# Attention's take-outs first in two queues, and the convolution's output projection in two halves of the contraction

## Chip, cores and metric

The kernel runs on one core of one Trainium2 chip. The metric is the device time of one execution in microseconds; the time of a kernel is the median of several runs. One further execution is taken with the hardware profiler, and all rows of the trace come from it.

## What is computed

Two decoder layers on 512 tokens of width 1024, in float32. Cut to what matters here:

```python
h = h + attention(rms_norm(h))     # layer 0: 16 query heads, 2 key/value heads, window 128,
                                   # softmax with a learned sink per head, then @ w_o
h = h + moe(rms_norm(h))           # 32 experts, top group of 4, then 2 of its 8 experts
h = h + gated_short_conv(rms_norm(h))                 # layer 1
h = h + moe(rms_norm(h))
out = rms_norm(h)

def gated_short_conv(h, w_in, conv_w, w_out):
    b_gate, c_gate, u = split(h @ w_in, 3)            # w_in: 1024 x 3072
    z = c_gate * u
    conv = sum(shift(z, 2 - j) * conv_w[j] for j in range(3))
    return (b_gate * conv) @ w_out                    # w_out: 1024 x 1024, contraction over 1024
```

## The kernel before, in words

Five engines run in-order programs of their own and hand over by semaphores: PE (matmuls), DVE and ACT (elementwise work, both read PSUM), POOL and SP (SP issues nearly all DMAs, in order). A product of two float32 matrices that must be exact is made of three matmuls on rounded parts (split_product, L833): each operand is split into a high part, written by ACT (L634), and a low part, written by DVE (L1247).

**Attention** goes by 8 units u, a block of 128 queries and one key/value head (8 query heads) each. Per unit PE makes scores (att_scores, L881), transposes the probabilities in four steps (att_turn, L901), multiplies by the values (att_out, L914) into bank 6, and, one unit behind, projects the heads of unit u - 1 in two halves of the columns (project_heads, L833) into bank 7. PE's order in unit u: scores(u+2), turn(u) steps 0 and 1, project_heads(u-1) half 0, turn(u) steps 2 and 3, project_heads(u-1) half 1, att_out(u). att_out's result is taken out of bank 6 in two steps, ACT's high part (att_take_out, L678) and then DVE's low part (L1309), and project_heads waits for the second. The queues around it: DVE does att_bias(u+2) (scores plus bias and their maximum, L1281 and three small steps, L1285 to L1287), att_take_out(u-1), add_heads (h += bank 7, L1317), att_scale(u+1) (L1297 to L1302), add_heads; ACT does att_exp(u+1) (L650, L653), att_scale(u) (L664), att_take_out(u-1), att_turn(u) (copies of the transposes, L670). The last units also hold the first steps of the next norm: root (ACT, L591, L596) and norm_tile (DVE, L1201), turned by PE (turn_tile, L819).

**The expert stages** stream the weights of 32 experts through a ring of 8 slots of 2 MB, laid over the buffers big, small, arena and xt. SP fills a slot when the product that used it is done (load_experts, L411); the first 8 fills of a layer wait for what held the buffer before, by the list early_free. The products are L1063 (gate and up) and L1081 (down).

**The convolution** makes h @ w_in in 8 gate blocks j of 128 columns of each of the three gates: 72 matmuls into banks 3(j%2) to 3(j%2)+2. w_in comes in four quarters of 256 columns through big[0] and big[1], w_out behind them (L459). For each block ACT copies the c gate out (L793) and splits the weights of block j + 2; DVE makes z, the three-tap convolution and the product with the b gate (L1541 to L1546), writes its high and low parts into gated and gated_low (L1547, L1548, conv_ready) and splits block j + 2. w_out's eight row blocks are split behind gates 6 and 7. When the last gate's DVE steps are done, project multiplies: for each of 4 token tiles t and 2 halves of the columns, f = 2t + half, 24 matmuls over the whole contraction into bank 6 + f%2. DVE adds the bank to h (L1360, mix_used), ACT and DVE norm the tile, PE turns it (turn_tile) and makes the router's logits (L974), woven between the products.

## Time and profile before

| | |
|---|---|
| median of 3 runs | 1422.33 us (1418.08 to 1423.3) |
| the profiled execution | 1416.9 us, span 1415.0 us |
| PE busy | 1259.5 us, 89% of the span |
| DVE, ACT, POOL busy | 410.2, 325.6, 153.7 us |
| DMA | 456.17 MB, mean 322 GB/s |
| chain that ended last | PE 63%, DMA 26%, DVE 7%, ACT 2% |

The span in 40 equal slices of 35.4 us; a digit is a busy share in tenths, PEclk the granted clock of TensorE:

```profile
PE   5978798999999999988389998999999999998891
DVE  6454453112111111111445454321112111111114
ACT  3235542211211112111331121112122111211112
POOL 5650030000000000000000000201000000000000
PEclk8989999999999999999679999999999999999996
DMA  9200635999999999999922232399999999999995
```

Slices 1 to 7 are attention, 7 to 19 the first expert stage, 21 to 26 the convolution, 27 to 39 the second expert stage. In the timelines a row has start, length, engine, line, operation and operands, and in brackets the idle time of the engine before it and what ended it. A matmul's end is modelled, so its length overlaps the next one's; a short one of 128x512 is listed with 0.39 us and followed after 0.23.

### The profile page before, as it was taken

The numbers are of one execution on the slowest core, as the hardware profiler recorded it, in microseconds if no ns is written. First come the engines' busy times: TensorE is split into PE (matmuls) and PEld (weight loads), VectorE is DVE, ScalarE is ACT, GpSimd is POOL, SyncE is SP. The second block draws the span as 40 slices with busy tenths as digits, with TensorE's granted clock in tenths as the row PEclk, the third lists the DMA queues.
The fourth block names the chain that finished last, engine by engine and source line by source line (L and its number), as shares of the span: only waits on it lengthen the run. The fifth ranks groups of instructions, "written<-read, shape, count | busy, mean of one in ns | idle before, by whom it ended". The sixth has DMA issues, their size and how long they took to land.

```text
span 1415.0 us, 15354 instructions
## 1 busy us (share of the span) xinstructions
PE 1259.5 (89%) x6042; PEld 672.2 (48%) x6042; DVE 410.2 (29%) x871; ACT 325.6 (23%) x620; POOL 153.7 (11%) x125
## 2 busy tenths in 40 slices
PE   5978798999999999988389998999999999998891
PEld 4756564444443433333168886744444434333330
DVE  6454453112111111111445454321112111111114
ACT  3235542211211112111331121112122111211112
POOL 5650030000000000000000000201000000000000
PEclk8989999999999999999679999999999999999996
DMA  9200635999999999999922232399999999999995
GB/s 351 86 0 1 244 150 240 427 428 426 429 428 428 429 426 429 428 427 427 340 44 89 89 119 119 125 427 426 428 426 428 429 428 427 429 427 427 428 422 212
DMA packets 63859, 456.17 MB, mean 322 GB/s; under 512 B 14852, under 2 KB 30238, under 8 KB 39236
## 3 DMA queue, kind: packets, MB, share of 16 engines
q1 hardware_dynamic: 52436, 444.29, 75.4%
q0 software_dynamic: 5120, 8.41, 1.6%
q10 hardware_dynamic: 6256, 2.80, 0.8%
q8 instruction: 34, 0.56, 0.2%
q14 instruction: 13, 0.11, 0.0%
HBM read 444.96 MB, written 18.90 MB: 328 GB/s over the span
## 4 chain that ended last, share of the span: by engine, by line
PE 63%; DMA 26%; DVE 7%; ACT 2%; issue 1%; POOLq 0%; DVEq 0%; ACTq 0%
PE ps L833 20%; PE ps L1063 20%; PE ps L1081 11%; DMA xt<-in_moe_w_gate_up_dram 10%; DMA big<-in_moe_w_gate_up_dram 10%; PE ps L1040 6%; DMA xt<-in_moe_w_down_dram 5%; PE ps L1053 1%; DVE xr L1201 1%; PE ps L1072 1%; PE ps L974 1%; PE ps L1048 1%; PE ps L914 1%; PE ps L819 1%; PE ps L881 1%
## 5 line engine op out<-in xcount | busy, mean ns | idle before, releaser
L1063 PE MATMUL ps<-big,arena 128*64 128x512 f32 x1024 | 228.1, 594 | 21.4 <-DMA big<-in_moe_w_gate_up_dram 20.7
L1452 DVE TENSOR_TENSOR gain<-arena,ps 64x512 f32<-64x512 f32 x64 | 68.7, 1073 | 432.9 <-ACT arena L721 432.9
L528 POOL DMA_INDIRECT rows<-arena x64 | 62.5, 977 | 880.6 <-DVE arena L1478 880.6
L721 ACT ACTIVATE arena<-ps 64x512 f32<-64x512 f32 x64 | 37.7, 590 | 518.7 <-PE ps L1063 518.7
L1063 PEld LDWEIGHTS ps<-big,arena 128*64 128x64 f32 x1024 | 72.3, 137 | 171.5 <-issue 136.2
L1063 PE MATMUL ps<-small,arena 128*64 128x512 f32 x512 | 114.9, 594 | 10.6 <-DMA small<-in_moe_w_gate_up_dram 10.6
L833 PE MATMUL ps<-xt_parts,small_parts 128*128 128x512 f32 x288 | 113.9, 405 | 6.9 <-DVE big L1260 5.4
L1081 PE MATMUL ps<-big,arena 128*64 128x512 f32 x512 | 116.9, 598 | 0.0
L833 PE MATMUL ps<-xr_parts,small_parts 128*128 128x512 f32 x272 | 108.5, 399 | 0.0
L833 PE MATMUL ps<-xt_parts,big_parts 128*128 128x512 f32 x256 | 101.6, 397 | 0.0
L1040 PE MATMUL ps<-arena_parts 128*128 128x512 f32 x256 | 83.6, 408 | 3.1 <-DVE arena_parts L1448 3.1
L1040 PE MATMUL ps<-xr_parts,arena_parts 128*128 128x512 f32 x256 | 80.0, 394 | 0.0
L1063 PEld LDWEIGHTS ps<-small,arena 128*64 128x64 f32 x512 | 36.1, 137 | 86.4 <-issue 67.5
L1478 DVE COPY arena<-ps 128x512 f32<-128x512 f32 x64 | 44.3, 692 | 96.4 <-PE ps L1081 96.0
L833 PEld LDWEIGHTS ps<-xt_parts,small_parts 128*128 128x128 f32 x288 | 56.5, 196 | 20.5 <-issue 6.8
L1081 PEld LDWEIGHTS ps<-big,arena 128*64 128x64 f32 x512 | 33.9, 136 | 63.1 <-issue 63.1
L1063 PE MATMUL ps<-arena 128*64 128x512 f32 x256 | 57.8, 594 | 5.3 <-DMA arena<-in_moe_w_gate_up_dram 5.3
L1477 DVE CAST arena<-arena 128x2 int32<-128x2 f32 x32 | 5.4, 169 | 196.9 <-PE ps L1081 196.9
L1063 PE MATMUL ps<-xt,arena 128*64 128x512 f32 x256 | 57.9, 594 | 5.1 <-DMA xt<-in_moe_w_gate_up_dram 5.1
L707 ACT ACTIVATE arena<-ps 128x512 f32<-128x512 f32 x64 | 34.7, 594 | 113.9 <-PE ps L1040 113.9
L819 PE MATMUL ps<-ident,xr 128*128 128x128 f32 x128 | 23.1, 342 | 40.9 <-DVE xr L1201 40.9
L1081 PE MATMUL ps<-small,arena 128*64 128x512 f32 x256 | 58.5, 598 | 0.8 <-DMA small<-in_moe_w_down_dram 0.8
(169 smaller groups left out, 1518.5 us busy)
## 6 DMA issues: line engine op xcount, KB each, us to landing
big<-in_moe_w_gate_up_dram SPq DMA_DIRECT2D x64, 2048.0 KB, 29.0
small<-in_moe_w_gate_up_dram SPq DMA_DIRECT2D x32, 2048.0 KB, 29.6
big<-in_moe_w_down_dram SPq DMA_DIRECT2D x32, 2048.0 KB, 32.8
xt<-in_moe_w_gate_up_dram SPq DMA_DIRECT2D x16, 2048.0 KB, 29.8
arena<-in_moe_w_gate_up_dram SPq DMA_DIRECT2D x16, 2048.0 KB, 30.1
small<-in_moe_w_down_dram SPq DMA_DIRECT2D x16, 2048.0 KB, 32.8
arena<-in_moe_w_down_dram SPq DMA_DIRECT2D x8, 2048.0 KB, 32.7
xt<-in_moe_w_down_dram SPq DMA_DIRECT2D x8, 2048.0 KB, 34.7
```

The source lines that it names most:

```text
L528: nc.gpsimd.indirect_dma_start(out=rows_dram[l], out_offset=bass.IndirectOffsetOnAxis(ap=where[:, j:j + 1], axis=0), in_=y_rows[:, j, :], ...
L707: nc.scalar.activation(picked[:, half * HALF:(half + 1) * HALF], ps[half][:], ACT.Copy)\
L721: nc.scalar.activation(silu[BLOCK:P, j, :], ps[2 + j][0:BLOCK, :], ACT.Silu).then_inc(S.silu_ready, 1)
L819: mm = nc.tensor.transpose(ps[f % 4][:, a * P:(a + 1) * P], xr[:, t, d * P:(d + 1) * P], ident[:])
L833: mm = nc.tensor.matmul(bank, parts(a), parts(b), start=start and a is left and b is right, stop=stop and a is left_low)
L881: mm = nc.tensor.matmul(ps[bank][:, col:col + hi * P], queries(n)[r0:r0 + HD, j, :], keys[r0:r0 + HD, g, (TT - 1 - n) * P:(TT - 1 - n + hi ...
L914: mm = nc.tensor.matmul(ps[6][half * HD:(half + 1) * HD, :], values[:, TT - 1 - n + c, g * HD:(g + 1) * HD], probsT[:, half * 4:half * 4 + ...
L1040: mm = nc.tensor.matmul(ps[half][:], parts(sel[:, t].rearrange("p j s -> p (j s)")), parts(x[:, t, half * HALF:(half + 1) * HALF]), start= ...
L1063: mm = nc.tensor.matmul(ps[2 + j][half * BLOCK:(half + 1) * BLOCK, :], xg[:, k, j * BLOCK:(j + 1) * BLOCK], w[:, a, half * FF:(half + 1) * ...
L1081: mm = nc.tensor.matmul(ps[6 + j][half * BLOCK:(half + 1) * BLOCK, :], hidT[:, j, k, :], w[:, k, half * HALF:(half + 1) * HALF], start=(k ...
L1452: V.tensor_tensor(hid[BLOCK:P, j, :].rearrange("q (k p) -> q p k", p=P), silu[BLOCK:P, j, :].rearrange("q (p k) -> q p k", p=P), ps[2 + j] ...
L1478: V.tensor_copy(y_rows[:, j, :], ps[6 + j][:]).then_inc(S.row_ready[j], 1)
```

## The change

1. Attention. On DVE att_take_out(u-1) stands ahead of att_bias(u+2). On ACT it stands first in the unit; att_exp(u+1) is cut in two halves of four heads, each ahead of two of the four copies of att_turn(u), and att_scale(u+1) comes last. Before the first unit, ACT scales unit 0 ahead of exp(1). At the end norm_tile(1,1) and root(1,1) stand ahead of the last take-out.
2. Convolution. The contraction of the output projection is cut in two. The first half (gate blocks 0 to 3) is multiplied behind gate block 5 (tile 0), 6 (tile 1) and 7 (tiles 2 and 3), and DVE adds it to h (add_first_half); project then multiplies the second half and adds again. w_out comes in two parts, its first half into rows of big that quarters 0 and 1 of w_in leave free, ahead of quarter 2 in SP's queue. Its splits stand behind gates 3, 6 and 7.
3. Expert ring of layer 1: the slots are in another order, with other early releases.
4. ACT's Square writes its unused output to another place (squares_at), since the arena is laid out anew.

```diff
-gated = cut(DT, T)
-gated_low = cut(DT, T)
+gated_parts = cut(2, 2, FT, T)
...
+out_high = cut(2, D)
...
 ring = [[halves[1][0], small[:, 0], halves[0][1], halves[0][0], late_slot, halves[1][1], small[:, 1], xt_slot],
-        [*halves[1], *halves[0], small[:, 0], small[:, 1], late_slot, xt_slot]]
+        [*halves[1], halves[0][1], small[:, 1], late_slot, halves[0][0], small[:, 0], xt_slot]]
...
+def first_half_bank(f):
+    return ps[half_banks[f]][:]
+half_banks = [6, 7, 6, 7, 6, 7, 0, 1]
...
 def out_weights(k):
-    at = 2 * CONV_W + k * D if k < 2 else (k - 2) * D
-    return big[:, QUARTERS % BIG_SLOTS, k, :], spare[:, at:at + D]
...
+    if k < 2:
+        return big[:, 0, 6 + k, :], spare[:, 2 * CONV_W + k * D:2 * CONV_W + (k + 1) * D]
+    if k < FT:
+        return big[:, 1, 4 + k, :], out_high[:, k - 2, :]
+    return big[:, 0, k - FT, :], spare[:, (k - FT) * D:(k - FT + 1) * D]
...
+SPLIT_ORDER = [("in", 0), ("in", 1), ("in", 2), ("in", 3), ("in", 4), ("in", 5),
+               ("out", 0), ("out", 1), ("out", 2), ("out", 3), ("in", 6), ("in", 7),
+               ("out", 4), ("out", 5), ("out", 6), ("out", 7)]
+def out_splits(j):
+    return {3: range(FT), DT - 2: range(FT, DT - 1), DT - 1: range(DT - 1, DT)}.get(j, [])
+def conv_split_at(what, n):
+    return CONV_SPLIT + SPLIT_ORDER.index((what, n))
...
             [(mix_ps, 4 * TT)] * 2 + [(logits_ps, TT)] if l == 0 else \
-            [(gates_ps, DT)] * 2 + [(mix_ps, 6 * TT)] * 5 + [(logits_ps, 2 * TT)]
+            [(gates_ps, DT)] + [(mix_ps, 6 * TT)] * 4 + [(mix_ps, 8 * TT)] * 2 + [(logits_ps, 2 * TT)]
...
+        if q == BIG_SLOTS:
+            for s in range(2):
+                sp.dma_start(big[:, s, 6:8], w_out[0, 2 * s * P:2 * (s + 1) * P, :].rearrange("(k p) n -> p k n", p=P))\
+                    .then_inc(w_out_in, 16)
...
     sp.wait_ge(gates_ps, (QUARTERS - BIG_SLOTS + 1) * QC // P)
-    sp.dma_start(big[:, QUARTERS % BIG_SLOTS], w_out[0].rearrange("(k p) n -> p k n", p=P)).then_inc(w_out_in, 16)
+    sp.dma_start(big[:, 0, 0:FT], w_out[0, FT * P:D, :].rearrange("(k p) n -> p k n", p=P)).then_inc(w_out_in, 16)
...
-            act.wait_ge(mix_used, TT * (i + 1) + 2 * t + 2)
+            act.wait_ge(mix_used, 4 * TT * (i // 2) + 2 * TT + 2 * t + 2)
...
-        nc.scalar.activation(x_high[:, t] if i % 2 else squares_at, h[:, t, :], ACT.Square,
+        nc.scalar.activation(squares_at, h[:, t, :], ACT.Square,
...
-    def att_exp(u):
+    def att_exp(u, half):
         b = u % 3
-        act.wait_ge(peak_ready, u + 1)
         hi = P if unit(u)[0] == 0 else 2 * P
-        nc.scalar.activation(sink_e[:, b, :], sink_e[:, b, :], ACT.Exp).then_inc(sink_ready, 1)
-        for k in range(HG):
+        if half == 0:
+            act.wait_ge(peak_ready, u + 1)
+            nc.scalar.activation(sink_e[:, b, :], sink_e[:, b, :], ACT.Exp).then_inc(sink_ready, 1)
+        for k in range(half * HG // 2, (half + 1) * HG // 2):
...
-    att_exp(0)
+    att_exp(0, 0)
+    att_exp(0, 1)
+    att_scale(0)
     for u in range(U):
-        if u + 1 < U:
-            att_exp(u + 1)
-        att_scale(u)
         if u >= 1:
             att_take_out(u - 1)
-        if u == U - 1:
+        if u + 1 < U:
+            att_exp(u + 1, 0)
+        att_turn(u, (0, 1))
+        if u + 1 < U:
+            att_exp(u + 1, 1)
+        else:
             root(1, 0)
-        att_turn(u)
+        att_turn(u, (2, 3))
+        if u + 1 < U:
+            att_scale(u + 1)
+    root(1, 1)
     att_take_out(U - 1)
-    for t in range(1, TT):
+    take_turned(1, 0)
+    for t in range(2, TT):
         root(1, t)
         take_turned(1, t - 1)
     take_turned(1, TT - 1)
...
+    def split_out(j):
+        for k in out_splits(j):
+            act.wait_ge(w_out_in, 16 * 2 if k < FT else 16 * 3)
+            if k >= FT:
+                act.wait_ge(gates_ps, DT - 1 if k < DT - 1 else DT)
             split_high(*out_weights(k))
...
-        if j == DT - 2:
-            act.wait_ge(w_out_in, 16)
-            split_out(range(5))
-        if j == DT - 1:
-            split_out(range(5, DT))
+        split_out(j)
...
-            for ks in ([range(5), range(5, DT)] if t == 0 else [range(DT)]):
+            for ks in ([range(FT, DT - 1), range(DT - 1, DT)] if t == 0 else [range(FT, DT)]):
                 for half in range(2):
                     f = 2 * t + half
-                    if f >= 2:
-                        pe.wait_ge(mix_used, first + f - 1)
+                    pe.wait_ge(mix_used, first + f - (1 if f >= 2 else 3))
                     for k in ks:
                         mm = product(ps[6 + f % 2][:], t, half, k)
                     if k == DT - 1:
...
+    def conv_product(bank, t, half, k):
+        if t == 0 and half == 0:
+            pe.wait_ge(w_split, conv_split_at("out", k) + 1)
+        w, high = out_weights(k)
...
-        pe.wait_ge(w_split, CONV_SPLIT + j + 1)
+        pe.wait_ge(w_split, conv_split_at("in", j) + 1)
...
+        if j == 5:
+            pe.wait_ge(conv_ready, FT)
+        for t in {5: [0], 6: [1], 7: [2, 3]}.get(j, []):
+            for half in range(2):
+                f = 2 * t + half
+                if t == TT - 1:
+                    pe.wait_ge(conv_ready, DT - 1)
+                elif t >= 1:
+                    pe.wait_ge(mix_used, 4 * TT + f - 1)
+                for k in range(FT):
+                    mm = conv_product(first_half_bank(f), t, half, k)
+                mm.then_inc(mix_ps, 1)
     pe.wait_ge(conv_ready, DT)
-    project(4 * TT, 3, conv_product)
+    project(6 * TT, 3, conv_product)
...
     take_queries(4, ps[7])
-    att_scale(0)
+    att_scale(0, (0, 1))
     att_bias(2)
     take_queries(5, ps[7])
+    att_scale(1, (0,))
     take_queries(6, ps[7])
-    att_scale(1)
+    att_scale(1, (1,))
     take_queries(7, ps[7])
     dve.wait_ge(h_biased, TT)
     for u in range(1, U):
         g, t = divmod(u - 1, TT)
+        att_take_out(u - 1)
         if u + 2 < U:
             att_bias(u + 2)
-        att_take_out(u - 1)
         add_heads(g, t, 0)
         if u + 1 < U:
-            att_scale(u + 1)
+            att_scale(u + 1, (0, 1))
         else:
             norm_tile(1, 0)
         add_heads(g, t, 1)
+    norm_tile(1, 1)
     att_take_out(U - 1)
-    norm_tile(1, 1)
     take_turned(1, 0)
...
-                dve.wait_ge(mix_ps, 2 * TT * (l + 1) + f + 1)
+                dve.wait_ge(mix_ps, 4 * TT * l + 2 * TT + f + 1)
...
+    def add_first_half(t):
+        for half in range(2):
+            f = 2 * t + half
+            dve.wait_ge(mix_ps, 4 * TT + f + 1)
+            hs = h[:, t, half * HALF:(half + 1) * HALF]
+            V.tensor_tensor(hs, first_half_bank(f), hs, ALU.add).then_inc(mix_used, 1)
...
     for j in range(DT):
         b = j % 2
+        if j == DT - 1:
+            add_first_half(1)
...
-            split_low(CONV_SPLIT + j + 2, *conv_weights(j + 2))
-        for k in (range(5) if j == DT - 2 else range(5, DT) if j == DT - 1 else []):
-            split_low(CONV_SPLIT + DT + k, *out_weights(k))
+            split_low(conv_split_at("in", j + 2), *conv_weights(j + 2))
+        for k in out_splits(j):
+            split_low(conv_split_at("out", k), *out_weights(k))
+        for t in {6: [0], 7: [2, 3]}.get(j, []):
+            add_first_half(t)
```

mix_ps and mix_used count 16 in attention, 8 in the first half and 8 in the second, where they counted 8 for the whole projection; root, add_mix and early_free are adapted to that.

## Rows read from the trace of the kernel before

**Rows 1.** Chain that ended last, in order of time: start, length, what.

```profile
229.49 13.95 PE ps L1063 x64
...
679.02 3.68 PE ps L1081 x16
...
856.53 18.04 PE ps L833 x72
...
932.35 13.95 PE ps L1063 x64
...
1382.91 3.68 PE ps L1081 x16
```

**Rows 2.** Waits of PE, 98 to 200 us: total, times, longest.

```profile
PE ps L833 <- DVE xr_parts L1309: 14.1, 7, 4.1
PE ps L833 <- issue: 2.4, 1, 2.4
PE ps L819 <- DVE xr L1201: 1.0, 1, 1.0
```

**Rows 3.** Timeline of PE, first projection matmul of attention units 4 and 7.

```profile
147.86 0.47 PE L833 MATMUL ps<-small_parts,xt_parts 128*128 128x512 f32 x1 [2.91 <-DVE xr_parts L1309]
...
184.37 0.47 PE L833 MATMUL ps<-small_parts,xt_parts 128*128 128x512 f32 x1 [0.49 <-DVE xr_parts L1309]
```

**Rows 4.** Timeline of DVE in unit 4.

```profile
143.66 0.42 DVE L1281 CUSTOM_DVE_ANT_0 arena<-ps,arena 128x256 f32<-128x256 f32 x1 [2.36 <-PE ps L881]
...
147.03 0.68 DVE L1309 TENSOR_TENSOR xr_parts<-ps,xt_parts 128x512 fp32r<-128x512 f32 x1
```

**Rows 5.** Groups by line, ACT and DVE, 128 to 170 us: busy us, mean ns.

```profile
L653 ACT ACTIVATE big<-big,arena 128x256 f32<-128x256 f32 x8 | 3.9, 502 | 0.0
L670 ACT ACTIVATE arena<-ps 128x512 f32<-128x512 f32 x12 | 6.5, 595 | 17.9 <-PE ps L901 17.9
...
L664 ACT ACTIVATE big<-big,arena 128x256 f32<-128x256 f32 x4 | 1.7, 498 | 0.0
...
L1302 DVE TENSOR_TENSOR big<-big,arena 128x1024 f32<-128x1024 f32 x1 | 1.2, 1226 | 0.0
```

**Rows 6.** Stretches: length, engines' busy us, then PEclk, DMA share, GB/s.

```profile
105.60:109.00 3.40, 3.33 (x9) 2.67 (x10) 0.02 (x1) 0.00 (x0) 0.00 (x0) 0.56 0.00 0
173.00:177.00 4.00, 4.00 (x13) 3.02 (x12) 0.00 (x0) 0.00 (x0) 0.00 (x0) 0.57 0.99 422
856.50:860.50 4.00, 3.97 (x11) 3.21 (x12) 3.50 (x3) 0.00 (x0) 0.00 (x0) 0.62 1.00 426
```

**Rows 7.** Timelines of ACT, DVE and PE at gates 6 and 7.

```profile
835.26 4.84 ACT L634 ACTIVATE small_parts<-big 128x1024 fp32r<-128x1024 f32 x5
...
835.47 0.69 DVE L1541 TENSOR_TENSOR arena<-arena,ps 128x512 f32<-128x512 f32 x1 [8.23 <-ACT arena L793]
...
840.20 5.77 DVE L1247 TENSOR_TENSOR big_parts<-big,small_parts 128x1024 fp32r<-128x1024 f32 x5
851.79 0.69 DVE L1541 TENSOR_TENSOR arena<-arena,ps 128x512 f32<-128x512 f32 x1 [5.83 <-ACT arena L793]
...
856.53 0.80 PE L833 MATMUL ps<-small_parts,arena_parts 128*128 128x512 f32 x1 [5.48 <-DVE arena_parts L1548]
```

**Rows 8.** Timeline of DVE behind the projection of tile 0.

```profile
869.16 0.69 DVE L1360 TENSOR_TENSOR h<-ps,h 128x512 f32<-128x512 f32 x1 [1.35 <-PE ps L833]
871.47 0.16 DVE L1194 RECIPROCAL rstd<-rstd 128x1 f32<-128x1 f32 x1 [1.61 <-ACT rstd L596]
871.67 2.07 DVE L1201 SCALAR_TENSOR_TENSOR xr<-h,rstd,gain 128x1024 f32<-128x1024 f32 x1
```

**Rows 9.** Timelines of DVE and POOL at the end of attention.

```profile
195.25 3.16 DVE L1201 SCALAR_TENSOR_TENSOR xr<-h,rstd,gain 128x1024 f32<-128x1024 f32 x1
...
194.21 2.40 POOL L542 TENSOR_TENSOR xr_parts<-xr,arena_parts 128x1024 fp32r<-128x1024 f32 x1
```

**Rows 10.** Timeline of SP's issues at the end of the convolution.

```profile
851.08 57.84 SPq L411 DMA_DIRECT2D big<-in_moe_w_gate_up_dram  x4
```

More of the change, by code:

```diff
@@ L665, in att_scale, with att_turn @@
                                          scale=rden[:, b, k:k + 1]).then_inc(scaled_act, 1)
-            def att_turn(u):
-                for f in range(4):
+            def att_turn(u, fs):
+                for f in fs:
                     act.wait_ge(pT_ps, 4 * u + f + 1)
@@ L775, in split_conv @@
                 split_high(*conv_weights(j))
-            def split_out(ks):
-                for k in ks:
-                    out_weights_wait(act, k)
+            def split_out(j):
[3 more added lines that the diff above has]
+                        act.wait_ge(gates_ps, DT - 1 if k < DT - 1 else DT)
                     split_high(*out_weights(k))
@@ L1154, in _ @@
             turn(2)
+            def conv_product(bank, t, half, k):
+                if t == 0 and half == 0:
+                    pe.wait_ge(w_split, conv_split_at("out", k) + 1)
+                w, high = out_weights(k)
+                cols = slice(half * HALF, (half + 1) * HALF)
+                rows = slice(t * P, (t + 1) * P)
+                return split_product(bank, gated(k)[:, rows], gated_low(k)[:, rows], high[:, cols], w[:, cols],
+                                     k % FT == 0, k % FT == FT - 1)
             for j in range(DT):
                 w, high = conv_weights(j)
-                pe.wait_ge(w_split, CONV_SPLIT + j + 1)
+                pe.wait_ge(w_split, conv_split_at("in", j) + 1)
                 if j >= 2:
@@ L1164, in _ @@
                 mm.then_inc(gates_ps, 1)
-            def conv_product(bank, t, half, k):
-                if t == 0 and half == 0:
-                    pe.wait_ge(w_split, CONV_SPLIT + DT + k + 1)
-                w, high = out_weights(k)
-                cols = slice(half * HALF, (half + 1) * HALF)
-                rows = slice(t * P, (t + 1) * P)
-                return split_product(bank, gated[:, k, rows], gated_low[:, k, rows], high[:, cols], w[:, cols],
-                                     k == 0, k == DT - 1)
+                if j == 5:
[10 more added lines that the diff above has]
+                        mm.then_inc(mix_ps, 1)
             pe.wait_ge(conv_ready, DT)
-            project(4 * TT, 3, conv_product)
+            project(6 * TT, 3, conv_product)
             router(1)
@@ L1293, in att_scale @@
                 dve.wait_ge(sink_ready, u + 1)
-                for half in range(2):
+                for half in halves:
                     heads = slice(half * 4, half * 4 + 4)
@@ L1357, in add @@
                             take_turned(2 * l + 1, t - 1)
-                        dve.wait_ge(mix_ps, 2 * TT * (l + 1) + f + 1)
+                        dve.wait_ge(mix_ps, 4 * TT * l + 2 * TT + f + 1)
                         hs = h[:, t, half * HALF:(half + 1) * HALF]
                         V.tensor_tensor(hs, ps[6 + f % 2][:], hs, ALU.add).then_inc(mix_used, 1)
-                    dve.wait_ge(mix_used, 2 * TT * (l + 1) + 2 * t + 2)
+                    dve.wait_ge(mix_used, 4 * TT * l + 2 * TT + 2 * t + 2)
                 return add
@@ L1546, in _ @@
                 step(V.tensor_tensor(conv, conv, ps[3 * b][:], ALU.mult))
[L1547 to L1548 removed]
+                step(V.tensor_copy(parts(gated(j)), conv))
+                V.tensor_tensor(parts(gated_low(j)), conv, parts(gated(j)), ALU.subtract).then_inc(conv_ready, 1)
                 dve.wait_ge(conv_ready, j + 1)
                 if j + 2 < DT:
[L1551 to L1553 removed]
+                    split_low(conv_split_at("in", j + 2), *conv_weights(j + 2))
[3 more added lines that the diff above has]
+                    add_first_half(t)
             norm(3, add_mix(1))
```

11 lines of the change are left out of this document (5 added, 6 removed).

## Prediction

> **What bounds the kernel now.** I read the chain that ended last first, in order of time, because it cuts the run into stages with different limits. From 229.49 to 679.02 (first expert layer) and from 932.35 to 1382.91 (second) it runs through expert products and, from the second half on, waits for expert weights [rows 1]: there the DMA is the limit, and I take such a stage as a block of fixed length behind its first product. The blocks are 679.02 - 229.49 = 449.53 us and 1382.91 - 932.35 = 450.56 us. So the change is worth what it moves the first expert product of each layer, plus what it changes in a block. The two stretches that it edits lie ahead: attention (to 229.49) and the convolution (to 932.35).
>
> In attention the waits of PE come next: 14.1 us in 7 waits for the take-out on DVE (L1309), and 2.4 us in one before a project_heads, with no releaser named, which by the code is the same wait (unit 5) [rows 2]. The timelines say why. In unit 4 PE has scores and transposes done near 145.0 and starts project_heads at 147.86, after 2.91 us [rows 3]. ACT's take-out stands behind exp and scale in its queue. DVE's stood behind att_bias, which began at 143.66 when the scores were there, and ran only at 147.03 [rows 4].
>
> In the convolution the chain is the gate blocks' and the projection's matmuls (8 x 72 and 192 by the code), with one stop of PE, 5.48 us before 856.53, for the last gate's DVE steps [rows 7]. A gate block of 72 matmuls takes 851.79 - 835.47 = 16.32 us, 0.227 us each at full clock [rows 7].
>
> **Attention, step by step.** With the take-outs first on ACT and DVE, the path from att_out's end to project_heads is ACT 0.6, DVE 0.7 and three hand-overs. Together that is 1.5 us. Unit 7, where nothing stands ahead of the take-outs and PE has only 1 us of transposes beside them, shows it: 0.49 us of wait are left [rows 3]. Units 1 to 5 have scores and transposes of over 2 us beside it, so their waits go to zero; unit 6, unit 7 and the last product keep 0.49 each. The waits sum to 14.1 + 2.4 = 16.5, so 16.5 - 1.5 = 15.0 us go.
>
> What is late next, counted from att_out's end in a middle unit: DVE takes out to 1.4, att_bias (2.9 + 0.6) to 4.9, the add of the first half at 5.8, scale (one step of 1.2 and four small ones) to 8.4. ACT takes out to 0.7, exp's first half (one small step, four of 3.9 / 8 = 0.49) to 2.8, two copies (0.54 each) to 4.1, exp's second half to 6.0, the other two copies, released by PE's transposes at about 6.7, to 7.2, scale (1.7) to 10.1 [rows 5]. PE's own work is 11.5 (10 for the shortest). att_out needs the copies at 9.5, the next unit's transposes need scale's first half at 13.4 and its second at 17. So PE stays the limit, with 2 us to spare at the tightest point. The exps are now queued behind a take-out that waits for PE, and PE's transposes wait for them; this slack is their cover, and without it they cost what is missing per unit. In unit 1 the add (behind att_bias and its GpSimd delays) should hold the second half by 0.5 us.
>
> PE's clock: behind the longest of these waits (4.1 us [rows 2], unit 1) the stretch 105.6 to 109.0 had a granted clock of 0.56, and behind unit 6's the stretch 173 to 177 had 0.57 [rows 6]. Losses of 3.4 x 0.44 + 4 x 0.43 = 3.2 us, at the 1.2 GHz level. I take the whole as regained; the bounds are 0 and 3.2.
>
> The end: norm_tile(1,1) moves ahead of DVE's last take-out. It then runs from 192.1, before GpSimd's subtraction (194.21) starts, in the 2.07 us that the same step takes alone, in place of the 3.16 that it took beside it [rows 8, 9]. The take-out comes 0.5 us later, the wait of 1.0 before turn_tile(1,1) goes [rows 2], and the following steps come about 0.7 us earlier in all. The Trainium skill (SBUF — State Buffer, Who interferes with whom) has it that a VectorE instruction with two SBUF inputs and a GpSimd one that reads SBUF block each other by issue order; these rows agree. By it this edit would be worth up to the whole 1.1 us, which moves the sum by 0.4.
>
> Attention: -15.0 + 0.5 - 3.2 - 0.7 = **-18.4 us** (bounds -14 to -20). The first layer's ring is then loaded no later relative to its first product: its seven early slots are released by events that move along, so its block stays at 449.5.
>
> **Convolution.** The product work is the same: 8 x 12 + 8 x 12 matmuls for 192. Loads: 2 MB of w_out go ahead of quarter 2 of w_in in SP's queue, and so delay it by some 5 us (5.2 to 12.8 was the landing time of such issues); DVE's split of block 4 ends near 778 and PE takes it at 786, so nothing is lost. The first four w_out splits, 4 x 0.97 on ACT and 4 x 1.15 on DVE [rows 7], fill the idle 8 us of DVE behind gate 3. add_first_half adds 8 DVE adds of 0.69 [rows 8]; 4 lie behind products, 4 behind the last gate, all while PE multiplies.
>
> The gain: behind block 7 PE has tiles 2 and 3, 48 x 0.227 = 10.9 us, where it stood 5.48. Gone are the stop and the slow matmuls after it: 72 took 18.04 against 16.32 [rows 1], about 1.6 without the pipeline's tail, with the clock at 0.62 [rows 6]. Together -7.0.
>
> The new wait: tile 1's first half, behind block 6, goes into bank 6, which still holds tile 0's. PE waits for mix_used 17, the add of tile 0. That add stands in DVE's queue at the end of gate 6, which can't begin before block 6 ends. Queued ahead of it: the gate's steps (its first begins at 835.47, 0.7 behind the block's end at 834.8, and the splits behind its last at 840.20: 5.4 us), then three splits of 1.15 (5.77 for 5), then the add itself, 0.69, and 0.1 to PE: 5.4 + 3.5 + 0.7 + 0.1 = **9.7 us** [rows 7, 8]. Behind the waiting PE stand tile 1, block 7 and all after it. DVE's splits wait for ACT's, 0.6 + 3 x 0.97 after the block, which is in time. A stop of 9.7 us costs at least the slow start of the 5.5 us one, 1.6 us. Together +11.3.
>
> The second half, 12 matmuls (2.7 us) for a bank instead of 24 (5.4), turns the norm into a wait. From a product's end to xr: the add begins 0.2 later, then 0.7, ACT's root 1.6, DVE 2.3 (0.2 and 2.07) [rows 8], 4.8 us. Before, PE had 5.4 (tile 0) or more beside it. Now turn_tile(0) waits 1.8, the next two 0.3 each. Together +2.4.
>
> Convolution: -7.0 + 11.3 + 2.4 = +6.7; written out from block to block I get tile 3's last product at 914.5 instead of 907.9, so **+6.6 us** (bounds +4, if the adds overlap better, to +10, with a second loss of clock).
>
> **Second expert block.** SP could issue two slots at 851.08 and then stood for 57.84 us [rows 10]. Now it issues one there, four with the first half done and two at the end; all eight are in SBUF before the first expert product. The first block (449.53) is the case in which they were, so **-1.0 us** (0 to -1.5). Three slots more beside the projection are otherwise worth nothing: the ring is full anyway until PE frees a slot.
>
> **Sum.** -18.4 + 6.6 - 1.0 = -12.8. Span 1415.0 to 1402.2. The profiled execution was 1416.9, 1.9 above its span, which gives 1404.1; it lay 5.4 below the median of the three runs, 1422.33. For a median of runs I take 1422.33 - 12.8 = 1409.5.
>
> **Rivals.** (A) The bank is free in time, and PE does not stop behind block 6. For it: two banks in turn. Against: the order of the DVE program, above. Then -18.4 - 7.0 + 2.4 - 1.0 = -24.0, 1398. The Trainium skill (Perfetto Trace Analysis, Matmuls) says that independent groups rotating through banks let the evacuation of one overlap the next group's matmuls; read by it alone this would happen. No row here shows an add of a first half; the trace bears out only that a released bank costs no wait.
> (B) ACT becomes the limit of a unit: exps behind the take-out push its last copies past the second half's end, and att_out waits. The slack is 2 us; were it missed by 1.4 us in each of six units, 8 us of the 18.4 are lost: -4.4, 1418. Against: ACT's busy time is about 8.6 of 11.5 us.
> (C) Slower: PE stays at 1.2 GHz after the 9.7 us stop, held there by the short stops of the second half. 24 + 72 + 48 + 96 = 240 matmuls follow, 0.2 us dearer each: 48 us, so 1422.3 - 12.8 + 48, about 1458. It is slower than before from 64 of these matmuls on. Against: after the 5.48 us stop the full clock was back in about 4 us: 11 matmuls there, where 17 fit at full clock, and only 1.7 us lost in 72 [rows 1, 6].
> (D) The moves don't act in attention, since PE's true limit there is another: 0 + 6.6 - 1.0, 1428.
>
> **Chances.** Forecast 0.69, A 0.09, B 0.14, C 0.03, D 0.05. Under 0.5% (7.1 us) this kernel's runs can't tell a change from none. The forecast's own range is 1402 to 1417, from the bounds above and the spread of the three runs; with A at one end and B at the other, 1398 to 1418. Faster by over 0.5%: most of the forecast and A, 0.77. Within: B and the rest of the forecast, 0.16. Slower: 0.07.
>
> **What would show it.** Waits of PE for L1309's successor of about 0.5 us, three times, in place of 16.5 us; first expert product near 211; behind gate block 6 one stop of 9 to 10 us, ended by a DVE add of h; none behind block 7; waits of 1 to 2 us before the first turned tile of the second half; first to last expert product 449 to 450 us in both layers; SP issuing four ring slots together before the second half. Wrong if PE stops longer than 1 us in units 2 to 6, or not at all behind block 6.

## Result, and the profile after

| kernel | median us | ratio to before, 95% interval | span of the profiled execution |
|---|---|---|---|
| before | 1420.2 (4 runs, 1417.94 to 1423.3) | | 1415.0 |
| after | 1404.05 (4 runs, 1401.89 to 1406.87) | 0.9886 [0.9856, 0.9916] | 1400.2 |

The change makes the kernel 16.2 us faster by the medians; the two profiled executions differ by 14.8 us.

The page of after, its parts 2 (granted clock in 40 slices) and 4 (chain by engine):

```profile
PEclk9999999999999999999599989999999999999996
...
PE 63%; DMA 27%; DVE 8%; ACT 1%; issue 1%; POOLq 0%; DVEq 0%; ACTq 0%
```

The shares hardly move; in the clock the 5 is the norm ahead of the convolution, and the 8 behind it the stop told of below. The chain in order of time (start, length, what) has the same stages as [rows 1]:

```profile
209.96 13.95 PE ps L1094 x64
...
659.45 3.68 PE ps L1112 x16
...
698.12 121.63 PE ps L865 x528
825.21 3.50 DVE big_parts L1291 x3
829.36 40.30 PE ps L865 x165
...
918.46 13.95 PE ps L1094 x64
...
1367.83 3.68 PE ps L1112 x16
```

Cut at the first and last expert product of each layer, for these two and for the kernels of the experiments that need it:

| us | before | after | att_only | conv_only | add_first | ring_late |
|---|---|---|---|---|---|---|
| to the first expert product | 229.49 | 209.96 | 208.40 | 234.08 | 208.23 | 213.06 |
| first block | 449.53 | 449.49 | 449.46 | 449.48 | 449.55 | 449.53 |
| norm, convolution, router | 253.33 | 259.01 | 253.15 | 260.61 | 248.96 | 261.02 |
| second block | 450.56 | 449.37 | 450.77 | 449.37 | 449.38 | 455.68 |

After against before: -19.5 in attention, +5.7 in the convolution, -1.2 in the second block and 0.3 more behind the last product make -14.8. The first block did not move.

Two of these stages hold a difference that is no work of the change. The 16 products of the pick, the last PE work of a router, take about 3.9 us at a granted clock of 1.00 and 5.5 us at a mean of 0.70. In attention they were slow in after and fast in before (3.91 us) and att_only (3.89); behind the convolution they were fast in after (3.87 us) and slow in before (5.49). The row of after in attention:

```profile
201.95 5.49 PE ps L1071 x16
```

With equal picks the change gives -21.1 in attention and +7.3 in the convolution, which are the values of att_only and conv_only; the 1.6 us cancel in the sum.

**Attention.** PE's waits from 80 to 200 us (total, times, longest), of the kernel after:

```profile
PE ps L865 <- DVE xr_parts L1353: 1.6, 3, 0.6
PE ps L865 <- DVE h L1361: 0.9, 2, 0.5
```

L1353 is the take-out, L1309 of before: 1.6 us in three waits where there were 16.5 in eight [rows 2]. DVE's timeline shows the take-out standing ahead of att_bias, and the product that waited 2.91 us [rows 3] starting without a pause, in PE's timeline:

```profile
131.86 0.69 DVE L1353 TENSOR_TENSOR xr_parts<-ps,xt_parts 128x512 fp32r<-128x512 f32 x1 [1.81 <-ACT xt_parts L704]
132.46 0.41 DVE L1325 CUSTOM_DVE_ANT_0 arena<-ps,arena 128x256 f32<-128x256 f32 x1
```
```profile
133.45 0.47 PE L865 MATMUL ps<-small_parts,xt_parts 128*128 128x512 f32 x1
```

**Convolution.** PE's waits from 820 to 920 us, then DVE at gate 6 and PE's first matmul after the stop, then a stretch behind it (the last three columns are PEclk, DMA share and GB/s):

```profile
PE ps L865 <- DVE h L1588: 9.6, 1, 9.6
PE ps L851 <- DVE xr L1245: 1.7, 2, 1.4
```
```profile
825.21 3.50 DVE L1291 TENSOR_TENSOR big_parts<-big,small_parts 128x1024 fp32r<-128x1024 f32 x3
828.62 1.28 DVE L1588 TENSOR_TENSOR h<-ps,h 128x512 f32<-128x512 f32 x2
...
829.36 0.80 PE L865 MATMUL ps<-small_parts,arena_parts 128*128 128x512 f32 x1 [9.61 <-DVE h L1588]
```
```profile
829.30:833.50 4.20, 4.14 (x10) 3.28 (x11) 0.60 (x2) 0.00 (x0) 0.00 (x0) 0.50 0.00 0
```

This is the predicted stop: the bank of tile 0's first half comes free only when the add has had its turn behind the gate's six steps and three splits. No stop is left behind gate block 7. The price can be read from ACT's c gates, which follow a block's end at once: 853.93 - 819.78 = 34.15 us between those of blocks 6 and 7 hold 9.6 of stop, tile 1's 24 matmuls (5.4) and block 7 (16.3). The last 2.8 are matmuls behind the stop at a granted clock of 0.50, the 1.2 GHz level. It was 1.00 before the stop:

```profile
819.78 0.60 ACT L829 ACTIVATE arena<-ps 128x512 f32<-128x512 f32 x1 [18.55 <-PE ps L865]
...
853.93 0.60 ACT L829 ACTIVATE arena<-ps 128x512 f32<-128x512 f32 x1 [30.72 <-PE ps L865]
```

**Second block.** SP issues one transfer at 853.93, behind gate block 7, four together from 864.91, when the first half is done, and the rest from 895.84 on, all before PE frees the first slot near 922:

```profile
853.93 0.34 SPq L432 DMA_DIRECT2D big<-in_moe_w_gate_up_dram  x1
...
864.91 0.82 SPq L432 DMA_DIRECT2D big<-in_moe_w_gate_up_dram  x2
...
866.25 0.51 SPq L432 DMA_DIRECT2D arena<-in_moe_w_down_dram  x1
...
895.84 0.33 SPq L432 DMA_DIRECT2D big<-in_moe_w_down_dram  x1
```

### The profile page after: what moved, and what is told of

Same layout as the page of the kernel before. It is cut to its first block, busy times and chain, and to the rows that moved or that the text cites. A ratio compares the mean times of both kernels' runs of the same rounds, so it can differ in the third digit from the quotient of the medians.

```text
span 1400.2 us, 15372 instructions
## 1 busy us (share of the span) xinstructions
PE 1255.3 (90%) x6042; PEld 669.7 (48%) x6042; DVE 414.9 (30%) x879; ACT 326.3 (23%) x620; POOL 154.1 (11%) x125
## 4 chain that ended last, share of the span: by engine, by line
PE 63%; DMA 27%; DVE 8%; ACT 1%; issue 1%; POOLq 0%; DVEq 0%; ACTq 0%
PE ps L1094 20%; PE ps L865 19%; PE ps L1112 11%; DMA xt<-in_moe_w_gate_up_dram 10%; PE ps L1071 6%; DMA xt<-in_moe_w_down_dram 5%; DMA small<-in_moe_w_gate_up_dram 5%; DMA big<-in_moe_w_gate_up_dram 5%; DVE xr L1245 2%; PE ps L1084 1%; PE ps L1103 1%; PE ps L1079 1%; PE ps L946 1%; PE ps L851 1%; PE ps L1006 1%
## 5 line engine op out<-in xcount | busy, mean ns | idle before, releaser
L1094 PE MATMUL ps<-big,arena 128*64 128x512 f32 x1024 | 229.1, 594 | 20.6 <-DMA big<-in_moe_w_gate_up_dram 20.0
```

The costliest lines, as they stand in the source:

```text
L1094: mm = nc.tensor.matmul(ps[2 + j][half * BLOCK:(half + 1) * BLOCK, :], xg[:, k, j * BLOCK:(j + 1) * BLOCK], w[:, a, half * FF:(half + 1) * ...
```

## Experiments 1: the parts apart

**att_only**: the kernel before with the attention part alone (the hunks of att_exp, att_turn, the two take-outs and norm_tile's place, with the buffer of root's squares).

> The kernel before with the attention part of the change alone. In the changed kernel the first expert product came at 209.96 us, 19.5 us earlier than before, and the convolution from the last expert product of layer 0 to the first of layer 1 took 259.0 us against 253.3. Theory (the two parts add up): the first expert product stays at 210 to 211, PE keeps waits for a take-out of about 0.5 us only, the convolution stage falls back to 253 to 255, and the second expert block to 450.5. Span 1415.0 - 19.5 = about 1395.5, ratio to before 0.986. Rival (a part of the attention gain came from the new memory layout or from the early w_out): the first expert product later than 213. Rival (the gain is eaten later, since the stages behind were paced by something else): ratio above 0.992.

Measured: 1397.24 us, ratio 0.9848 [0.9817, 0.9879]. The first expert product came at 208.40, 21.1 earlier; the rest of the run was as before (253.15 and 450.77). The attention part is worth the whole gain and more.

**conv_only**: the kernel before with all the rest of the change.

> The kernel before with the convolution part and the ring of layer 1 alone. Theory: the stop of 9.6 us behind gate block 6 and the slow matmuls after it (+11.2), less the stop and slow matmuls behind block 7 (-7.0), plus waits in the second half (+1.7 to +2.4), less 1.0 to 1.2 in the second expert block: +4.5 to +5.5 us, span 1419.5 to 1420.5, ratio 1.002 to 1.005. Rival (the convolution part was a gain, and attention brought more than its waits): ratio under 0.999. Rival (the parts only cost together): ratio 1.000 with no stop behind block 6.

Measured: 1424.51 us over 10 runs, 1.0038 [1.0022, 1.0054]. The stage grew by 7.3 us, the second block shrank by 1.2. That makes 6.1, more than the 4.5 to 5.5 expected; PE has the same stop of 9.6 us and the same 1.7 us of waits in the second half as in after, and where the rest lies was not traced. So the convolution part alone makes the kernel slower, though by less than 0.5%. The 4.6 us before the first expert product of this execution are no work of the edit, which touches nothing there: the last section names them.

**add_first**: after, with DVE's add of tile 0 ahead of gate 6's steps.

```diff
-                if j == DT - 1:
-                    add_first_half(1)
+                if j >= DT - 2:
+                    add_first_half(j - (DT - 2))
...
-                for t in {6: [0], 7: [2, 3]}.get(j, []):
+                for t in {7: [2, 3]}.get(j, []):
```

> The changed kernel, with one order changed on DVE: the add of tile 0's first half stands ahead of gate 6's steps instead of behind them and behind three splits. Theory (the stop behind gate block 6 is the queue of DVE and nothing else): the stop of 9.6 us goes, the matmuls behind it run at full clock, and nothing else is late, since tile 0's product is done 16 us before block 6 ends: -9.6 - 1.6 = -11.2 us against the changed kernel, span about 1389, ratio to before 0.981. Rival (the stop moves on, since gates 6 and 7 or the splits of w_out on DVE are then late for block 7's tiles or for the second half): a new stop behind block 7 and less than 5 us gained. Rival (the clock is lost anyway): -9.6 alone.

Measured: 1393.54 us, 0.9822 [0.9791, 0.9852]. The two longest waits of PE from 800 to 905 us:

```profile
PE ps L851 <- DVE xr L1245: 1.7, 2, 1.4
PE ps L1071 <- DVE arena_parts L1493: 1.5, 1, 1.5
```

No wait for L1588 is among them or left below them, and the chain runs from the first gate block to the projection in one piece (in this kernel, start and length):

```profile
696.50 159.86 PE ps L865 x693
```

The stage is 10.05 us shorter than after's and 11.65 shorter than conv_only's (whose picks ran at the same clock as add_first's); 11.3 was the predicted price of the stop, 11.2 the expected gain. The same adds of the same halves, in another place of DVE's queue: so the stop is DVE's order and nothing else, and without it the split in two halves gains 253.33 - 248.96 = 4.4 us over before instead of losing 7.3 (all at the same clock of the picks).

**ring_late**: after, with four of layer 1's early ring slots released at the end of the second half instead of the first.

```diff
-                    [(gates_ps, DT)] + [(mix_ps, 6 * TT)] * 4 + [(mix_ps, 8 * TT)] * 2 + [(logits_ps, 2 * TT)]
+                    [(gates_ps, DT)] + [(mix_ps, 8 * TT)] * 6 + [(logits_ps, 2 * TT)]
```

> The changed kernel, with four slots of the second layer's ring released when the second half of the projection is done, not the first. My prediction gave these slots no worth beyond 1.0 us, as the ring is full before the first expert product either way. Counted out with the changed kernel's rows: seven slots at 4.9 us behind the projection's end at 895.8 end at 930, and PE frees its first slot at 922.1. Theory (all eight must be in by then, or the DMA, which limits the stage, starts its stream late): the second expert block grows from 449.4 by 930 - 922 = about 8 us, to 457, ratio to before about 0.994. Rival (a ring filled late costs nothing, since PE is at first slower than the DMA): block 449.5 to 451 and ratio 0.989.

Measured: 1412.52 us over 8 runs, 0.9948 [0.993, 0.9966]. SP issues one early slot at 857.50 and the next ones only from 899.38; the first slot is free again at 927.30:

```profile
899.38 0.82 SPq L432 DMA_DIRECT2D big<-in_moe_w_gate_up_dram  x2
...
927.30 3.76 SPq L432 DMA_DIRECT2D big<-in_moe_w_gate_up_dram  x2
```

The second block took 455.68, 6.3 more. Loads that start 28 us before the first slot is freed do not fill the ring, and what is missing is paid at the weights' rate. Before lacked 1.2 us of it. After's 449.37 is as short as the first blocks, 449.46 to 449.55 in all six kernels, so slots released still earlier have nothing to gain there.

## Experiments 2: attention's orders

These four tell apart which order made the gain, how much slack ACT has (rival B), and what norm_tile's place is worth.

**act_order**: the kernel before with ACT's program of after alone. **dve_order**: the kernel before with this edit of DVE alone:

```diff
+                att_take_out(u - 1)
                 att_bias(u + 2)
-                att_take_out(u - 1)
```

> The kernel before with ACT's new order in attention alone (take-out first, exp in two halves, scale last); DVE's take-out still stands behind att_bias. What is compared is when PE starts the first router logits: 202.6 us before, 181.5 with the whole change. Theory (DVE's queue ends the wait wherever PE has scores, ACT's only in unit 6): the waits for the take-out stay at 12 to 14 us, unit 6 falls from 1.82 to 0.49, logits at 200 to 201.5. Rival (ACT's queue was the cause): waits under 5 us, logits before 192.

> The kernel before with one step moved: DVE's take-out ahead of att_bias; ACT's take-out still behind exp and scale. Worked out from rows of before: in unit 4 ACT's take-out ended at 144.0, so DVE's would end at 144.7, before PE's transposes at 145.0; but once PE is faster, ACT's copies, exp and scale (1.1 + 4.1 + 1.7 us) end only about 13 us into a unit of 10 to 11.5, and its take-out comes 1.5 us late in the shorter units. Theory: this step alone gives 9 to 12 of the 21 us, waits of PE of 0.5 to 2 us left in units 2, 4, 5, 6, logits at 190 to 193. Rival (both orders are needed, since DVE now stands still until ACT's take-out and att_bias is late): logits after 198. Rival (DVE's order is all): logits before 184.

Measured: act_order 1416.61 us over 8 runs, 0.9974 [0.9958, 0.999]; dve_order 1401.45 over 2, 0.9861 [0.9777, 0.9945]. Waits of PE for the take-out, first of act_order, then of dve_order:

```profile
PE ps L842 <- DVE xr_parts L1318: 12.8, 7, 4.1
PE ps L842 <- issue: 2.4, 1, 2.4
```
```profile
PE ps L833 <- DVE xr_parts L1309: 2.8, 4, 1.7
```

With ACT's order alone, among the take-out's waits only unit 6's gets shorter (1.82 to 0.49), where DVE has no att_bias ahead of the take-out, and the router's logits start at 202.91 against 202.44. That is later than the 200 to 201.5 expected, but this start can't be held against before's: between 100 and 184 us the part of the full clock that was missing sums to 8.5 us in this execution and to 3.4 in before's (one less the granted clock, times 4 us, over all stretches of 4 us), and it was the slowest of the 8 runs. The ratio, below 1 with its interval, says that ACT's order alone gives a few us. With DVE's alone the logits start at 185.24, which is 17.2 of the 21.1 us. I had given DVE's order 9 to 12, taking ACT's take-out behind exp and scale to be as late as DVE's behind att_bias. It was late by at most 1.7 us, and in four units only. DVE's order is most of the change. The last 3.9 us are ACT's order and norm_tile's place together, which dve_order leaves out too; the place alone is worth 1.1 (norm_after).

**exp_whole**: after, with both halves of att_exp ahead of att_turn's first two copies. **norm_after**: after, with DVE's last take-out ahead of norm_tile(1, 1) again.

> The changed kernel with exp(u+1) in one piece, all eight heads ahead of the copies of the transposes. ACT's first two copies then end 5.9 us after att_out's end instead of 4.1, PE's third and fourth transposes need them at 5.3 to 6.2 in units with scores and at 4.3 in unit 6. Theory (the cut in two halves is worth little): 0 to 0.5 us per unit and about 1.5 in unit 6, logits 1 to 4 us later than 181.5. Rival (the cut carries the gain, since late copies also push the scale and the next unit): logits later than 188.

> The changed kernel with DVE's norm_tile(1,1) back behind its last take-out. Theory: it meets GpSimd's subtraction again and takes 3.2 us instead of 2.1; the last projection of the heads starts 0.5 us earlier and turn_tile(1,1) waits 1 us; logits 0.5 to 1.0 us later than 181.5. Rival (the order there doesn't matter): within 0.2 us.

Measured: exp_whole 1406.11 us, 0.9894 [0.9825, 0.9963]; norm_after 1405.75, 0.9891 [0.9823, 0.996], both over 2 runs. By the medians neither can be told from after; the traces can, by the start of the logits (181.31 in after): 182.46 and 182.41. exp_whole has two waits of PE for ACT's copies (L696), 1.3 us together. Pushing 2 us of exp ahead of the copies costs 1.15 us in the whole of attention, so ACT has slack in nearly every unit. In norm_after the DVE and POOL timelines give the mechanism:

```profile
174.45 3.92 DVE L1245 SCALAR_TENSOR_TENSOR xr<-h,rstd,gain 128x1024 f32<-128x1024 f32 x1
...
174.17 2.40 POOL L567 TENSOR_TENSOR xr_parts<-xr,arena_parts 128x1024 fp32r<-128x1024 f32 x1
```

The norm step falls on GpSimd's subtraction and takes 3.92 us. In after it runs ahead of it:

```profile
171.94 2.04 DVE L1245 SCALAR_TENSOR_TENSOR xr<-h,rstd,gain 128x1024 f32<-128x1024 f32 x1
...
174.83 2.41 POOL L567 TENSOR_TENSOR xr_parts<-xr,arena_parts 128x1024 fp32r<-128x1024 f32 x1
```

Its place is worth 1.1 us. The PSUM take-out, which moved the other way, costs 0.69 in either place.

## Experiments 3: what is late next, and a faster version

All start from add_first, and aim at stretches where PE waits or runs at the lower clock between the stages. keep_busy(n), already in the kernel before, issues n matmuls of the identity that nobody reads (two of 128x512 each in the trace), to fill PE's idle time.

**turn_early**: PE turns tile 2 of the norm ahead of the logits of tiles 0 and 1.

```diff
+            turn_tile(1, 2)
             logits(0, 0)
             logits(0, 1)
-            turn_tile(1, 2)
```

> The kernel add_first, with PE's turn_tile(1,2) ahead of the router logits of tiles 0 and 1 instead of behind them. In add_first it starts 3.5 us behind the end of the last projection of the heads, though xr is there; DVE's last norm_tile stands behind the copy that waits for it. Theory (this transpose is on the path): turn_tile(1,3) and all behind it come 2.5 to 3.5 us earlier, so from the start of the last projection of the heads (174.6) to the first product of the pick 24.5 us instead of 27.3. Rival (the last norm waits for ACT's root and GpSimd, not for PE): 0 to 0.7 us. The clock can fall in this stretch, which cost 4.5 to 4.7 us in other runs (25.1 us from the logits to the pick against 20.6), and is read apart by the granted clock.

Measured: 1389.49 us over 2 runs, 0.9798 [0.9778, 0.9817]. From tile 1's turn to the first pick product 25.23 us against 24.43 in add_first: no gain there in this execution. From the start of the last projection of the heads it was 28.1 us where 24.5 were expected. Part of the reason is in PE's timeline; the fill work ran at half clock, and tile 3's turn, ready at 186.67, stood behind it:

```profile
186.27 3.52 PE L1013 MATMUL ps<-ident 128*128 128x512 f32 x4
189.59 1.22 PE L851 MATMUL ps<-ident,xr 128*128 128x128 f32 x8
```

Tile 3's norm step came earlier than in add_first (182.75 against 186.58), but it falls on a subtraction of GpSimd again. The rows of DVE and of GpSimd:

```profile
182.75 3.92 DVE L1245 SCALAR_TENSOR_TENSOR xr<-h,rstd,gain 128x1024 f32<-128x1024 f32 x1
...
182.54 2.34 POOL L567 TENSOR_TENSOR xr_parts<-xr,arena_parts 128x1024 fp32r<-128x1024 f32 x1
```

The median is 4.05 us under add_first's, the profiled execution only 1.3, 1.6 of which are the pick's clock behind the convolution, and the intervals overlap: a gain is not shown.

**warm_norm**: unread matmuls into a free bank while PE waits for the norm between the first expert stage and the convolution.

```diff
             experts(0)
-            turn(2)
+            keep_busy(20)
+            for t, busy in enumerate((2, 3, 1, 2)):
+                turn_tile(2, t, busy)    # busy unread matmuls behind the turn
```

> The kernel add_first, with matmuls that nobody reads (28 more, into an unused bank) while PE waits between the first expert stage and the first gate block. What is tested is what slow matmuls behind a stop cost. Theory: PE's clock is at its high level at the first gate block; the transposes take 1.1 instead of 1.97 us and the first 12 matmuls 0.23 instead of 0.43: from the last expert product of layer 0 to the end of gate block 0, 54.9 us fall by 3 to 3.5. Rival (the extra matmuls delay the transposes by what they save, since they stand ahead of them in order): -0.5 to +2 us.

Measured: 1391.22 us over 2 runs, 0.981 [0.979, 0.983]. One of the four turns and the first gate matmuls, first of add_first, then of warm_norm:

```profile
685.25 1.97 PE L851 MATMUL ps<-ident,xr 128*128 128x128 f32 x8 [2.06 <-DVE xr L1245]
...
696.50 0.77 PE L865 MATMUL ps<-xt_parts,small_parts 128*128 128x512 f32 x1 [1.46 <-DVE xr_parts L1254]
```
```profile
689.55 1.09 PE L851 MATMUL ps<-ident,xr 128*128 128x128 f32 x8 [1.23 <-DVE xr L1250]
...
700.08 0.47 PE L868 MATMUL ps<-xt_parts,small_parts 128*128 128x512 f32 x1
```

The turns take 1.09 instead of 1.97. From the last expert product to the first gate matmul it is 0.6 us less (38.13 against 38.72), and the gate and projection matmuls, 159.86 in one piece in add_first, take 157.49: 3.0 together, the lower end of what was expected. The medians (two runs here) leave it open, since the intervals of warm_norm and add_first overlap.

**best**: both. **best_2**: both, with the fill work moved: one group between the logits of tiles 0 and 1, and none ahead of tile 3's turn.

```diff
             logits(0, 0)
+            keep_busy(1)
             logits(0, 1)
             logits(0, 2)
-            keep_busy(2)
             turn_tile(1, 3)
```

> add_first with both: the early transpose and the matmuls that keep the clock. Theory (they add up): 5.5 to 6.5 us under add_first, median 1387 to 1388, ratio to before about 0.978. Rival (one of them does nothing): ratio 0.980 to 0.982.

> The kernel best, with the idle-time matmuls at the end of attention in another place: one call of keep_busy between the logits of tiles 0 and 1, and none of the two ahead of turn_tile(1,3). In turn_early xr of tile 3 was there at 186.7, but PE ran keep_busy at 1.2 GHz until 189.6, after three tiles of logits in a row. Theory (the clock falls in the row of 40-column matmuls, and the idle-time matmuls then stand in the way): from turn_tile(1,1) to the pick 22 to 23 us, against 26.9 in best, 25.2 in turn_early and 24.4 in add_first; ratio to before 0.975 to 0.978. Rival (the clock falls here all the same, by chance and from run to run): 24 to 26 us, and the ratio of best, 0.979.

Measured: best 1387.02 us (4 runs), 0.9789 [0.9764, 0.9813]; best_2 1386.15 (4 runs, 1384.33 to 1389.28), 0.9761 [0.9719, 0.9803]. In best_2 the stretch from tile 1's turn to the pick is 22.5 us (177.41 to 199.91), against 26.85 in best and 24.43 in add_first. The two can't be told apart by the medians. Nor is it shown that the moved fill work kept the clock up: turn_early and best have the same program of PE there, and in turn_early the first three tiles of logits took 5.45 us at a granted clock of 1.00, in best 6.87 us, with the clock falling. Both beat after, by 17 to 18 us and without any change of what is computed; of these, 10.5 are the one moved add.

## Why the prediction was right, and by how much its terms were off

The forecast was 1409.5 us and the median is 1404.05. Of the 5.5 us, 2.1 are the reference (the four runs of before have their median at 1420.2, not 1422.33) and 3.4 the change, 16.2 instead of 12.8 us; 14.8 in the profiled pair.

- **The DMA-bound blocks.** Right. The first did not move, the second by -1.2 against -1.0, and ring_late shows that it is the early slots that make it. SP issued four of them together at 864.91, with the first half done, as forecast. (The 57.84 us in which the prediction has SP stand before [rows 10] are the length of that whole row; the wait in it was 56.2.)
- **Attention's waits.** Right: 16.5 to 1.6, with 1.5 forecast, at the places named (units 6, 7 and the last product).
- **Attention's sum.** Predicted -18.4, measured -21.1 to the logits and -19.5 to the first expert product; -21.1 there too in att_only, whose pick ran at before's clock. Of these, 14.9 are the take-out's waits and 1.0 the one before turn_tile(1, 1). Waits for the adds of the heads cost 0.6 more (0.9 in two, 0.3 before), where the prediction put 0.5. The clock gives 3.4, where it put 3.2: from 100 to 184 us it was 1.00 throughout in after. Another 1.4 us lie ahead of the first projection of heads: att_out of unit 0 starts at 96.20 instead of 97.58. There the scores of the stretch 60 to 64 us ran at a granted clock of 0.60 in before, and at 1.00 in after; but it was 1.00 in conv_only too, which has before's attention, so most of this is a difference between executions and not the change. The last 1.0 is not traced. The undersized term is what comes back besides the waits. At the first expert product the pick's slow products leave 19.5 of the 21.1.
- **The order at the end.** Right: the norm step runs alone in 2.04 us, and its place is worth 1.1 us where 0.7 was forecast. The whole 1.1 is what the sentence drawn from the Trainium skill (SBUF — State Buffer, Who interferes with whom) gave, and 3.92 us beside a GpSimd subtraction, against 2.04 alone, agree with it.
- **Rival B** (ACT becomes the limit). Wrong, by exp_whole: even with the exps whole ahead of the copies the loss is 1.15 us, not 8.
- **The stop behind gate block 6.** 9.7 forecast, 9.6 measured, by the chain of DVE steps written out there. The slow matmuls after it were put at 1.6 us, the price of the 5.5 us stop, and cost 2.8 in after, but 1.8 behind the same stop in conv_only. The term was a lower bound by its own words, but used as the value; its size changes from one execution to the next (last section).
- **The second half's waits.** 2.4 forecast, 1.7 measured, in two waits instead of three.
- **The convolution's sum.** +6.6 forecast, +5.7 in this pair; but 1.6 us of that difference is the clock of the pick, and conv_only against before with equal picks gives +7.3. The forecast lies between. So the gain in attention was put 2.7 us too low and the loss here 0.7 too low; in the sum the two errors work against each other. The sign of this half of the change, a loss, is shown by conv_only's interval above 1, and att_only agrees: its slowest run (1397.84) is under after's fastest (1401.89), though the intervals of the two ratios overlap.
- **Rival A** (the bank is free in time, 1398). It did not happen, and add_first builds its state: 1393.5. The Trainium skill (Perfetto Trace Analysis, Matmuls) has groups that rotate through banks overlap the evacuation of one with the next group's matmuls. Here two banks rotated and PE stopped 9.6 us, since the evacuation stood 5.4 + 3.5 us deep in an in-order queue. Where page and trace differ, the trace decides; with the add first, it agrees with the page.
- **Rival C** (PE held at 1.2 GHz through the second half). Wrong: the stretch 833.5 to 837.5 already had a mean granted clock of 0.85. **Rival D** (nothing gained in attention). Wrong, by att_only.

## What to carry to other kernels

Read for each hand-over where the releasing instruction stands in its engine's queue: a 0.7 us step that frees the engine on the critical path belongs ahead of work that nobody waits for, and that alone was worth 17 us at one place (dve_order) and 10 at another (add_first). Rotating banks protect against the length of an evacuation, not against its place in a queue. A change in two parts is to be timed in two parts: here one gained 21 us, the other lost 6, and the sum hid it.

## What the hardware showed beyond that

**The clock fell in a stretch where PE was busy.** Behind attention, PE makes the router's logits as rows of 128x40 matmuls, between turned tiles. That stretch in dve_order (two rows) and in add_first (one row); length, PE's and the other engines' busy us, then the granted clock. It fell at the end of the first stretch, in which PE was counted busy for all of 4.00 us:

```profile
185.20:189.20 4.00, 4.00 (x35) 3.96 (x34) 0.69 (x1) 1.45 (x3) 2.40 (x2) 0.92 0.71 209
189.20:193.20 4.00, 3.12 (x16) 2.75 (x14) 2.31 (x3) 0.60 (x1) 2.24 (x1) 0.50 1.01 434
```
```profile
189.50:193.50 4.00, 3.12 (x24) 2.36 (x22) 1.23 (x2) 1.88 (x2) 3.15 (x2) 1.00 0.88 371
```

From the first logits matmul to the first pick product it took 20.6 us at full clock (before, act_order, att_only, after, add_first) and 25.1 to 25.4 where the clock fell (conv_only, ring_late, dve_order, exp_whole, norm_after, warm_norm). Nothing in the code there goes with it: before and conv_only have the same attention, and their first expert products lie at 229.49 and 234.08; after, add_first, ring_late and warm_norm have the same attention, and took 20.6, 20.6, 25.1 and 25.2. The 16 pick products behind the convolution have two lengths too, 5.46 to 5.49 us in before, att_only, conv_only, add_first and ring_late, 3.87 in after. That these 1.6 to 4.6 us make much of the spread between runs of one kernel (5 us in after's four) is an inference from two signs. Every run's mean granted clock is on record, and in the 19 runs of before beside att_only it was 0.966 to 0.970 in those under 1419 us and 0.960 in the slowest (1425.33). And of conv_only's ten runs four took 1421.2 to 1422.7 us and five 1425.3 to 1427.6. So where a few us matter, a stage is to be compared together with its clock.

**The price of a stop is more than its length, and is not the same each time.** Behind the 5.5 us stop, which four kernels share, the 72 matmuls that take 16.3 us at full clock took 17.96 to 18.05 in before, att_only and dve_order, and 19.52 in act_order: 1.6 to 1.7, or 3.2 us dearer.

```profile
856.76 19.52 PE ps L842 x72
```

Behind the 9.6 us stop the c gates of blocks 6 and 7 show it. In add_first, without the stop, they lie 21.8 us apart. With it they lie 34.1 apart in after and exp_whole, and 33.1 to 33.2 in conv_only, ring_late and norm_after, so the price was 2.7 or 1.7 to 1.8 us (by the sum of parts in after, 2.8). In conv_only:

```profile
844.97 0.60 ACT L820 ACTIVATE arena<-ps 128x512 f32<-128x512 f32 x1 [18.55 <-PE ps L856]
...
878.09 0.60 ACT L820 ACTIVATE arena<-ps 128x512 f32<-128x512 f32 x1 [29.68 <-PE ps L856]
```

So the price differs as much between executions of the same stop as between the two stops, and that it grows with the length is not shown. Behind the 38 us between the stages, in which PE mostly waits for the norm, warm_norm got 3.0 back by keeping PE busy with unread work in them. Such work pays where nothing useful can come due behind it, and costs where it can: in turn_early four matmuls of it, at the lower clock, held back a turned tile for 2.9 us (186.67 to 189.59).
